# Modulation products of four steps gathered in one row tile before they are turned into columns

## The chip, the cores and the metric

The kernel runs on one core of a Trainium2 chip. The time is the device time of one execution in microseconds (us). The engines are TensorE (PE, with its weight loads shown apart as PEld), VectorE (DVE), ScalarE (ACT), GpSimd (POOL) and SyncE (SP), which issues most DMAs. TensorE writes its results into eight PSUM banks of 128 partitions by 512 fp32 words.

## The reference, cut to what matters

Two blocks are computed one after the other: a first one of two layers (attention with a forget gate, convolutions, feed-forward) over 272 tokens, then a second one whose norms are modulated. The modulation vectors are what this case is about:

```python
N_MOD = 9                       # D_MODEL = 1024
ml = (jax.nn.silu(c) @ ada_w[l] + ada_b[l]).reshape(B, N_MOD, 1, D)
mc = (jax.nn.silu(c_ctx) @ ada_w[l] + ada_b[l]).reshape(N_MOD, 1, 1, D)
x = x + 0.5 * ml[:, 2] * _swiglu(_modulate(_rms(x, ffn1_norm[l]), ml[:, 0], ml[:, 1]), ffn1_w_in[l], ffn1_w_out[l])
h = h + 0.5 * mc[2] * _swiglu(_modulate(_rms(h, ffn1_norm[l]), mc[0], mc[1]), ffn1_w_in[l], ffn1_w_out[l])
...
```

So two vectors of 1024 (silu of c and of c_ctx) are multiplied by a matrix of 1024 x 9216. The rest of the kernel needs the results as columns, 128 features on the partitions: 72 tiles of 128 features, two columns each (tile MOD, seen flat as `modf`).

## The kernel before

Everything is fp32. Each engine has its own hand-written order of instructions; semaphores tie them together (`S.name`), and a small counter class turns them into waits on constants. A matmul of fp32 is two TensorE instructions in the trace.

**Where the modulation is computed.** The matrix of 9216 columns is cut into 18 steps of 512 columns (q = 0 to 17), each fed by two weight strips of 256 columns in the slots W[0] to W[3]. Steps 0 and 1 are in the attention of layer 0, steps 2 and 3 in that of layer 1, steps 4 to 17 in the first feed-forward of the second block (the modulated stage): one after each of its ten product groups and one after each of its four down-projections (`ada(g)`, g = 0 to 13, called as `extra` from `ffn`).

**What a step does.** In `ada_products` (L858) TensorE takes a bank and multiplies, for 8 blocks of 128 features and both strips, the stationary tile CC[:, k, :] of 32 columns by 256 columns of the strip. Only the first two of the 32 columns of CC hold data (written at L1888), the rest are zero. Block k goes to rows 32 * (k % 4) of the bank, so the product lies there in four partial sums of two rows each. `ada_rows` (L1765) on ScalarE copies the bank, 128 x 512, into the row tile AR (two buffers) and gives the bank back. `ada_columns` (L871) on TensorE multiplies each quarter of AR, 128 x 128, as stationary operand by SEL, whose two columns have ones at rows 0, 32, 64, 96 and 1, 33, 65, 97: that adds the partial sums and turns rows into columns, 8 columns in all. `ada_columns` (L1774) on ScalarE copies these into MOD.

**Order around it.** In the feed-forward stage the columns of step 3 + g are turned right after the products of step 4 + g (`ada_turn`, L1204 and L2088), so there the row copy of ScalarE has a whole step of time. In the last, g = 13, the columns of both 16 and 17 are turned. After them TensorE goes on with the sum of squares (`square_sum`, in `stat`, L749), which waits for VectorE's `x2_ready` (set at L2884), and the next norm hangs on it. In the layers both steps' products (L1089, L1090) come before `turn(6)`, and the columns are turned in `turn(6)` and `turn(7)` (L991), ahead of each head's three transposes (L998); ScalarE evicts these in `evict` (L1843, L1844) and then copies the columns (L1776). After `evict(6)` it squares rows (L1858). SyncE loads the output projection (`w_out`) into the same slots as soon as the products have released them. VectorE adds the bias and forms the gains in `modulation(pairs, ...)` (L2413), which first waits for a number of column copies.

Of the kernel before, what the change touches and what calls it, by code (L numbers as in the profile page):

```python
# [28 lines left out]
SW = 256  # L29
# [227 lines left out]
def first_and_second_block(nc, a, out):  # L257
# [4 lines left out]
    with ctx:  # L262
        def sb(name, shape, dt=F32):
            return ctx.enter_context(nc.sbuf_tensor(name, shape, dt))

        S = Semaphores(lambda name: ctx.enter_context(nc.semaphore(name)))
        bank = [ctx.enter_context(nc.psum_tensor(f"bank{b}", [P, 512], F32)) for b in range(8)]


        W = [sb(f"W{r}", [P, SK, SW]) for r in range(SLOTS)]  # L270

        ident = sb("ident", [P, P])
        mean_d = sb("mean_d", [P, P])
        mean_c = sb("mean_c", [P, P])
        mean_g = sb("mean_g", [P, P])
        SEL = sb("SEL", [P, 2])
        eps_rms = sb("eps_rms", [P, 1])
        eps_ln = sb("eps_ln", [P, 1])
        ones_row = sb("ones_row", [P, T1])
# [13 lines left out]
        MOD = sb("MOD", [P, NMOD, KD, 2])  # L293
        GS = sb("GS", [P, 3, KD, 2])
        GATE = sb("GATE", [P, 3, KD, 2])
        CC = sb("CC", [P, KD, 32])
        LBC = sb("LBC", [P, 4, 16])
        NB = sb("NB", [P, 16])
        MQB = sb("MQB", [P, 4])
# [142 lines left out]
        AR = cut(2, 2 * SW)  # L442
# [260 lines left out]
        def _(eng):  # L703
# [9 lines left out]
            def take(b):  # L713
                eng.wait_ge(S.free[b], p.next(S.free[b]))
# [141 lines left out]
                seven_products(n % 2, 4, P, (n % 4,), lambda i: WSM[n % 2][:, i], tokens, lambda i: sums[i],  # L856
                               tokens=each, halves=wait, swap=last)

            def ada_products(b, r):

                take(b)
                for half in range(2):
                    rr = (r + half) % 4
                    eng.wait_ge(S.land[rr], p.next(S.land[rr], 16))
                    for k in range(KD):
                        g = 32 * (k % 4)
                        last = mm(bank[b][g:g + 32, half * SW:(half + 1) * SW], CC[:, k, :], W[rr][:, k, 0:SW],  # L867
                                  start=k < 4, stop=k >= 4, skip_group_check=True)
                    last.then_inc(S.done[rr], p.inc(S.done[rr]))

            def ada_columns(o, q):  # L871

                eng.wait_ge(S.ada_rows, p.next(S.ada_rows))
                for n in range(4):
                    last = mm(o[:, 2 * n:2 * n + 2], AR[:, q % 2, n * P:(n + 1) * P], SEL[:, :], start=True, stop=True,  # L875
                              skip_group_check=True)
                return last

# [65 lines left out]
            for l in range(LAYERS):  # L944
# [46 lines left out]
                def turn(j):  # L991

                    eng.wait_ge(S.p_norm, p.next(S.p_norm))
                    take(6)
                    if j > 5:
                        ada_columns(bank[6][:, 384:392], l * 2 + j - 6)
                    for c in range(3):
                        last = eng.transpose(bank[6][:, c * P:(c + 1) * P], SP[j % 3][:, c * P:(c + 1) * P], ident[:, :])  # L998
                    last.then_inc(S.pt_full, p.inc(S.pt_full))
# [86 lines left out]
                scores(7)  # L1086
                if l == 0:
                    eng.wait_ge(S.cc, p.now(S.cc))
                ada_products(0, 2)  # L1089
                ada_products(1, 0)  # L1090
                turn(6)
                eng.wait_ge(S.vt, p.next(S.vt))
                weigh(2)
# [107 lines left out]
                    if extra:  # L1201
                        extra(10 + u)

            def ada_turn(q):  # L1204

                take(6)
                ada_columns(bank[6][:, 0:8], q).then_inc(S.ada_full, p.inc(S.ada_full))

            def ada(g):

                ada_products(5, 1)
                if g:
                    ada_turn(3 + g)
                if g == 13:
                    ada_turn(17)

            ffn(u2, 2 * SEQ, lambda g: 3 if g else 1, ada)
            square_sum(2 * SEQ)
# [489 lines left out]
        def _(eng):  # L1708
# [53 lines left out]
                    act(sn[:, i, :], bank[b][:, c:c + w], ACT.Copy).then_inc(S.snap, p.inc(S.snap))  # L1762
                p.skip(S.prod, 2)

            def ada_rows(b, r, q):  # L1765

                p.skip(S.done[r % 4])
                r = (r + 1) % 4
                eng.wait_ge(S.done[r], p.next(S.done[r]))
                act(AR[:, q % 2, :], bank[b][:, :], ACT.Copy).then_inc(S.ada_rows, p.inc(S.ada_rows))  # L1770
                eng.wait_ge(S.ada_rows, p.now(S.ada_rows))
                eng.sem_inc(S.free[b], 1)

            def ada_columns(o, q):  # L1774

                act(modf[:, 4 * q:4 * q + 4, :], o.rearrange("p (a b) -> p a b", a=4), ACT.Copy).then_inc(S.mod, p.inc(S.mod))  # L1776
                eng.wait_ge(S.mod, p.now(S.mod))

            for l in range(LAYERS):
# [61 lines left out]
                def evict(j):  # L1841
                    eng.wait_ge(S.pt_full, p.next(S.pt_full))
                    act(PT[:, j, 0:256], bank[6][:, 0:256], ACT.Copy)  # L1843
                    act(PT[:, j, 272:400], bank[6][:, 256:384], ACT.Copy).then_inc(S.pt_ready, p.inc(S.pt_ready))  # L1844
                    eng.wait_ge(S.pt_ready, p.now(S.pt_ready))
                    if j > 5:
                        ada_columns(bank[6][:, 384:392], l * 2 + j - 6)
                    eng.sem_inc(S.free[6], 1)

                def mixed(pair):  # L1850
# [34 lines left out]
                    eng.wait_ge(S.xn, p.next(S.xn))  # L1885
                    act(CS[:, t, :], CV[:, t, :], ACT.Silu, bias=PLs[l][:, C_LNB + t:C_LNB + t + 1]).then_inc(S.cact, p.inc(S.cact))
                if l == 0:
                    act(CC[:, :, 0:2], GS[:, 0, :, :], ACT.Silu).then_inc(S.cc, p.inc(S.cc))  # L1888
                tables(LOG_EXP)
                copies(2, SCX)  # L1890
                evict(2)
# [9 lines left out]
                copies(1, YC[:, 4:6, :])  # L1901
                evict(5)
                exps(7)
                ada_rows(0, 2, l * 2)
                ada_rows(1, 0, l * 2 + 1)
                evict(6)
                eng.wait_ge(S.ysc, p.next(S.ysc, 2))
                head_squares(HK[0:4])
# [176 lines left out]
                if not extra:  # L2085
                    finish(range(6, 8))

            def ada_turn(q):  # L2088

                eng.wait_ge(S.ada_full, p.next(S.ada_full))  # L2090
                ada_columns(bank[6][:, 0:8], q)
                eng.sem_inc(S.free[6], 1)

            def ada(g):

                ada_rows(5, 1, 4 + g)
                if g:
                    ada_turn(3 + g)
                if g == 13:
                    ada_turn(17)  # L2100

            ffn(2 * SEQ, lambda g: 3 if g else 1, 0, 0, ada)
            norm(2 * SEQ, 1, 3)
# [220 lines left out]
        def _(eng):  # L2324
# [22 lines left out]
            def constants():  # L2347

                eng.wait_ge(S.consts, p.next(S.consts))
                eng.memset(maskC[:, 0:SEQ], 0.0)  # L2350
                eng.tensor_reduce(maskC[:, SEQ:T1], H2[:, 0, 0:P].rearrange("p (j c) -> p c j", j=HEADS), AX_X, ALU.add)
                for n, at in enumerate((32, 64, 96)):
                    tt(SEL[:, :], SEL[:, :] if n else ident[:, 0:2], ident[:, at:at + 2], ALU.add).then_inc(S.order_dve, p.inc(S.order_dve))
                    eng.wait_ge(S.order_dve, p.now(S.order_dve))

            def par(c):
# [56 lines left out]
            def modulation(pairs, t0, t1, norm_at=(), gate_at=()):  # L2413

                eng.wait_ge(S.mod, p.next(S.mod, pairs))
                tt(modf[:, t0:t1, :], modf[:, t0:t1, :], P2[:, B_ADA + t0:B_ADA + t1].unsqueeze(2).to_broadcast([P, t1 - t0, 2]), ALU.add).then_inc(S.order_dve, p.inc(S.order_dve))
                eng.wait_ge(S.order_dve, p.now(S.order_dve))
                for n in norm_at:
                    gain, sc = norms_of[n]
                    ts(GS[:, n], MOD[:, sc], 1.0, None, ALU.add).then_inc(S.order_dve, p.inc(S.order_dve))  # L2420
                    eng.wait_ge(S.order_dve, p.now(S.order_dve))
                    tt(GS[:, n], GS[:, n], P2[:, gain:gain + KD].unsqueeze(2).to_broadcast([P, KD, 2]), ALU.mult).then_inc(S.order_dve, p.inc(S.order_dve))
                    eng.wait_ge(S.order_dve, p.now(S.order_dve))
                for n in gate_at:
# [30 lines left out]
            def context():  # L2455

                eng.wait_ge(S.sig, p.next(S.sig))
                tt(LBC[:, 1, :], LBC[:, 2, :], LBC[:, 3, :], ALU.add).then_inc(S.order_dve, p.inc(S.order_dve))
                eng.wait_ge(S.order_dve, p.now(S.order_dve))
                eng.reciprocal(LBC[:, 1, :], LBC[:, 1, :]).then_inc(S.order_dve, p.inc(S.order_dve))  # L2460
                eng.wait_ge(S.order_dve, p.now(S.order_dve))
                tt(LBC[:, 0, :], LBC[:, 2, :], LBC[:, 1, :], ALU.mult).then_inc(S.order_dve, p.inc(S.order_dve))
                eng.wait_ge(S.order_dve, p.now(S.order_dve))
                ts(LBC[:, 1, :], LBC[:, 0, :], -1.0, 1.0, ALU.mult, ALU.add).then_inc(S.order_dve, p.inc(S.order_dve))
                eng.wait_ge(S.order_dve, p.now(S.order_dve))
                modulation(4, 0, 16, norm_at=(0,))

            def context_norm():

# [414 lines left out]
                    eng.memset(tick[:, 0:1], 0.0).then_inc(S.x2_ready, p.inc(S.x2_ready))  # L2884
                    eng.wait_ge(S.x2_ready, p.now(S.x2_ready))

            ffn(2 * SEQ, lambda g: 3 if g else 1, 0, lambda: modulation(8, 16, 48, norm_at=(1,), gate_at=(0, 1)))
            norm(2 * SEQ, 1)
            modulation(6, 48, 72, norm_at=(2,), gate_at=(2,))

            for k in range(KD):
                eng.wait_ge(S.u, p.next(S.u))
# [369 lines left out]
```

## Time and profile before

| | |
|---|---|
| Median of 3 runs | 2059.34 us (2059.31 to 2059.37) |
| The profiled execution | 2057.46 us |
| its span, first to last instruction | 2055.7 us |
| mean granted clock | 0.998 of full speed |

TensorE is busy for 98% of the span by the page. The page gives each engine's busy time, the chain of work that ended last, and the costliest groups of instructions. A chain is followed back from the last instruction: at each step to whatever released it, or to the instruction before it on its engine. The waits list who waited for whom. The timeline merges instructions of one line that follow each other: start, duration, engine, line, operation, output tile and inputs, count, and in brackets the idle time of the engine before it and what ended it. Two timeline rows of TensorE can overlap slightly, since a matmul's end is pipelined under the next one; starts are the better measure.

### The profile page before, as it was taken

The page shows a single profiled execution, that of the slowest core. Times are in us where ns is not written, and L with a number is a line of the kernel's source. Part 1 is how long each engine was busy: PE and PEld are TensorE (multiplying, and loading weights), DVE is VectorE, ACT ScalarE, POOL GpSimd, SP SyncE. Part 2 cuts the span into 40 slices and gives each one's busy share as a digit, 9 for nine tenths or more (in the row PEclk, how much of TensorE's full clock was granted, in tenths as well). Part 3 has the DMA queues.
Part 4 walks back from the last instruction along what each step waited for, and adds up shares of the span by engine and source line. Part 5 has one row for each costly group of instructions (what it writes and reads, how often), then busy time and mean ns, then how long its engine had stood idle before and what let it go on. Part 6 is the DMA issues. An engine that isn't in the chain of part 4 may idle for free.

```text
span 2055.7 us, 31756 instructions
## 1 busy us (share of the span) xinstructions
PE 2023.5 (98%) x12969; PEld 1806.3 (88%) x12969; DVE 1079.0 (52%) x2170; ACT 569.3 (28%) x1366; POOL 175.9 (9%) x232
## 2 busy tenths in 40 slices
PE   9999999999999999999999999999999999999998
PEld 7868999977789998888888888888889889999998
DVE  5424987571278865333336235333245545776664
ACT  3344332223433313111111004322332323232212
POOL 5110340312013300000000001000000000000000
PEclk9999999999999999999999999999999999999999
DMA  6244454342444543444455336422212214444552
GB/s 191 95 156 146 165 171 155 107 145 97 159 162 146 194 134 101 151 145 152 149 172 167 98 100 193 128 85 83 82 62 82 62 54 131 165 144 165 172 182 77
DMA packets 274874, 273.63 MB, mean 133 GB/s; under 512 B 11023, under 2 KB 272379, under 8 KB 274731
## 3 DMA queue, kind: packets, MB, share of 16 engines
q1 hardware_dynamic: 272920, 267.65, 40.2%
q0 software_dynamic: 1216, 3.32, 0.5%
q8 instruction: 103, 1.69, 0.3%
q10 hardware_dynamic: 594, 0.65, 0.1%
q14 instruction: 41, 0.33, 0.0%
HBM read 270.38 MB, written 1.08 MB: 132 GB/s over the span
## 4 chain that ended last, share of the span: by engine, by line
PE 94%; DVE 3%; ACT 1%; DMA 1%; issue 1%; SPq 0%; DVEq 0%; ACTq 0%
PE bank L782 50%; PE bank L1224 11%; PE bank L769 8%; PE bank L1403 5%; PE bank L910 3%; PE bank L1417 2%; PE bank L969 2%; PE bank L1021 1%; PE bank L867 1%; PE bank L1468 1%; PE bank L1389 1%; PE bank L1430 1%; DMA W<-in_ada_w_dram 1%; PE bank L875 1%; PE bank L980 1%; PE bank L1156 1%
## 5 line engine op out<-in xcount | busy, mean ns | idle before, releaser
L782 PE MATMUL bank<-arena,SQ 128*128 128x136 f32 (+2 forms) x2176 | 341.5, 308 | 2.6 <-ACT arena L1762 2.6
L782 PEld LDWEIGHTS bank<-arena,SQ 128*128 128x128 f32 x2176 | 307.0, 191 | 19.8 <-ACT arena L1762 2.8
L782 PE MATMUL bank<-arena,W 128*128 128x136 f32 (+2 forms) x1824 | 272.6, 301 | 2.3 <-issue 2.1
L782 PEld LDWEIGHTS bank<-arena,W 128*128 128x128 f32 x1824 | 247.7, 191 | 13.6 <-issue 2.4
L1762 ACT ACTIVATE H<-bank 128x128 f32<-128x128 f32 (+1 forms) x260 | 82.4, 317 | 508.9 <-PE bank L782 508.8
L782 PE MATMUL bank<-U,W 128*128 128x136 f32 (+2 forms) x1296 | 194.4, 303 | 0.0
L782 PEld LDWEIGHTS bank<-U,W 128*128 128x128 f32 x1296 | 176.5, 191 | 8.5 <-issue 0.4
L769 PE MATMUL bank<-U,W 128*128 128x272 f32 (+2 forms) x608 | 140.6, 392 | 2.4 <-DVEq L2409 1.2
L769 PEld LDWEIGHTS bank<-U,W 128*128 128x128 f32 (+1 forms) x608 | 111.7, 185 | 30.0 <-issue 3.9
L782 PE MATMUL bank<-arena 128*128 128x136 f32 (+1 forms) x1024 | 124.1, 278 | 0.0
L782 PEld LDWEIGHTS bank<-arena 128*128 128x128 f32 x1024 | 120.6, 191 | 0.0
L2552 DVE TENSOR_TENSOR arena<-H,bank 128x128 f32<-128x128 f32 (+1 forms) x57 | 19.1, 334 | 160.1 <-ACT H L1762 160.1
L1224 PE MATMUL bank<-W,U 128*128 128x256 f32 (+1 forms) x512 | 100.5, 355 | 0.0
L782 PE MATMUL bank<-U,SQ 128*128 128x136 f32 (+2 forms) x608 | 98.2, 304 | 0.0
L1224 PEld LDWEIGHTS bank<-W,U 128*128 128x128 f32 x512 | 86.8, 190 | 11.5 <-issue 2.0
L1762 ACT ACTIVATE arena<-bank 128x136 f32<-128x136 f32 x176 | 49.2, 280 | 169.5 <-PE bank L782 169.5
L782 PEld LDWEIGHTS bank<-U,SQ 128*128 128x128 f32 x608 | 85.9, 191 | 4.1
L1224 PE MATMUL bank<-arena 128*128 128x256 f32 (+3 forms) x352 | 66.2, 332 | 0.0
L1674 POOL TENSOR_TENSOR SQ<-W 128x512 f32<-128x512 f32 x32 | 40.8, 1276 | 279.4 <-PE bank L782 279.4
L1224 PEld LDWEIGHTS bank<-arena 128*128 128x128 f32 (+2 forms) x352 | 52.2, 179 | 14.1 <-issue 4.0
L2703 DVE SCALAR_TENSOR_TENSOR arena<-arena,PL 128x270 f32<-128x270 f32 x72 | 61.8, 858 | 2.6
L910 PE MATMUL bank<-arena,W 128*128 128x272 f32 x256 | 60.3, 394 | 1.7 <-ACT arena L1752 1.7
(418 smaller groups left out, 3052.4 us busy)
## 6 DMA issues: line engine op xcount, KB each, us to landing
W<-in_ffn_w_up_dram SPq DMA_DIRECT2D x44, 1024.0 KB, 5.0
W<-in_ffn_w_in_dram SPq DMA_DIRECT2D x44, 1024.0 KB, 5.0
W<-in_ada_w_dram SPq DMA_DIRECT2D x36, 1024.0 KB, 6.5
W<-in_mix_w_in_dram SPq DMA_DIRECT2D x36, 1024.0 KB, 5.3
W<-in_w_in_dram SPq DMA_DIRECT2D x22, 1024.0 KB, 5.1
W<-in_ffn_w_down_dram SPq DMA_DIRECT2D x16, 1408.0 KB, 6.4
W<-in_ffn_w_out_dram SPq DMA_DIRECT2D x16, 1408.0 KB, 6.0
W<-in_w_out_dram SPq DMA_DIRECT2D x8, 1024.0 KB, 8.1
```

The costliest lines, as they stand in the source:

```text
L769: last = mm(bank[b][0:m, 0:n], W[r][:, kk, t * P:t * P + m], rhs(kk), start=kk == 0, stop=kk == k - 1)
L782: last = mm(o, a(k), b[:, k], start=not adds and k == 0, stop=k == kt - 1, skip_group_check=True)
L867: last = mm(bank[b][g:g + 32, half * SW:(half + 1) * SW], CC[:, k, :], W[rr][:, k, 0:SW], start=k < 4, stop=k >= 4, skip_group_check=True)
L875: last = mm(o[:, 2 * n:2 * n + 2], AR[:, q % 2, n * P:(n + 1) * P], SEL[:, :], start=True, stop=True, skip_group_check=True)
L910: return mm(bank[2 * (r % 2) + t][:, c0:c0 + n], W[r][:, k, t * P:(t + 1) * P], rhs(k), start=k == 0, stop=k == KD - 1, skip_group_check=True)
L969: last = mm(o, U[:, kk, t0:t0 + w], W[r][:, kk, 0:SW], start=kk == 0, stop=kk == KD - 1)
L1224: last = mm(o, x, y, start=i == 0, stop=i == n - 1 and bias is None, skip_group_check=True)
L1403: last = mm(bank[b][:, c:c + SEQ], W[r][:, k, t * P:(t + 1) * P], src[:, k, c:c + SEQ], start=k == 0, stop=k == KD - 1, skip_group_check=True)
L1417: last = mm(bank[b][:, c:c + SW], tok(k), W[r][:, k, :], start=k == 0, stop=k == KD - 1, skip_group_check=True)
L1674: eng.tensor_tensor(WS[n % 2][:, 0], part(1, 0), part(1, 1), ALU.add).then_inc(S.order_pool, p.inc(S.order_pool))
L1762: act(sn[:, i, :], bank[b][:, c:c + w], ACT.Copy).then_inc(S.snap, p.inc(S.snap))
L2703: stt(CZ[:, i, 2:], Z[:, g % 2, i, 0:T1 - 2], w(0), CZ[:, i, 2:], ALU.mult, ALU.add).then_inc(sem, p.inc(sem))
```

## The change

Up to four steps now add into one bank. Step i of a group of n uses CC shifted by two columns, so that its data fall on rows 2 i and 2 i + 1 of every group of 32; only the very first products carry the start flag. CC grows to 38 columns with the data in columns 6 and 7, SEL to 8 columns. One copy of the bank into AR then carries n steps, and one turning gives 8 n columns in four matmuls of 2 n. In the layers the two steps form one group, turned with head 7. In the feed-forward stage the groups are steps 0 to 3, 4 to 7, 8 to 11 and 12, 13 (g), turned in steps 4, 8, 12 and 13. The last is turned right after its own products.

```diff
-        SEL = sb("SEL", [P, 2])
+        SEL = sb("SEL", [P, 8])
-        CC = sb("CC", [P, KD, 32])
+        CC = sb("CC", [P, KD, 38])
...
-            def ada_products(b, r):
-
-                take(b)
+            def ada_products(b, r, i, n):
+
+                if i == 0:
+                    take(b)
                 for half in range(2):
                     rr = (r + half) % 4
                     eng.wait_ge(S.land[rr], p.next(S.land[rr], 16))
                     for k in range(KD):
                         g = 32 * (k % 4)
-                        last = mm(bank[b][g:g + 32, half * SW:(half + 1) * SW], CC[:, k, :], W[rr][:, k, 0:SW],
-                                  start=k < 4, stop=k >= 4, skip_group_check=True)
+                        last = mm(bank[b][g:g + 32, half * SW:(half + 1) * SW], CC[:, k, 6 - 2 * i:38 - 2 * i], W[rr][:, k, 0:SW],
+                                  start=i == half == 0 and k < 4, stop=i == n - 1 and k >= 4, skip_group_check=True)
                     last.then_inc(S.done[rr], p.inc(S.done[rr]))
-            def ada_columns(o, q):
+            def ada_columns(o, a, n):
                 eng.wait_ge(S.ada_rows, p.next(S.ada_rows))
-                for n in range(4):
-                    last = mm(o[:, 2 * n:2 * n + 2], AR[:, q % 2, n * P:(n + 1) * P], SEL[:, :], start=True, stop=True,
+                for j in range(4):
+                    last = mm(o[:, 2 * n * j:2 * n * (j + 1)], AR[:, a, j * P:(j + 1) * P], SEL[:, 0:2 * n], start=True, stop=True,
                               skip_group_check=True)
...
-                    if j > 5:
-                        ada_columns(bank[6][:, 384:392], l * 2 + j - 6)
+                    if j == 7:
+                        ada_columns(bank[6][:, 384:400], 0, 2)
...
-                ada_products(0, 2)
-                ada_products(1, 0)
+                ada_products(0, 2, 0, 2)
+                ada_products(0, 0, 1, 2)
...
             def ada(g):
-                ada_products(5, 1)
-                if g:
-                    ada_turn(3 + g)
+                ada_products(5, 1, g % 4, 2 if g > 11 else 4)
+                if g in (4, 8, 12):
+                    ada_turn(g // 4 - 1, 4)
                 if g == 13:
-                    ada_turn(17)
+                    ada_turn(3, 2)
...
-            def ada_rows(b, r, q):
-
-                p.skip(S.done[r % 4])
-                r = (r + 1) % 4
-                eng.wait_ge(S.done[r], p.next(S.done[r]))
-                act(AR[:, q % 2, :], bank[b][:, :], ACT.Copy).then_inc(S.ada_rows, p.inc(S.ada_rows))
+            def ada_rows(b, slots, a):
+
+                for r in slots:
+                    eng.wait_ge(S.done[r], p.next(S.done[r]))
+                act(AR[:, a, :], bank[b][:, :], ACT.Copy).then_inc(S.ada_rows, p.inc(S.ada_rows))
...
-                    if j > 5:
-                        ada_columns(bank[6][:, 384:392], l * 2 + j - 6)
+                    if j == 7:
+                        ada_columns(bank[6][:, 384:400], l * 2, 2)
...
-                ada_rows(0, 2, l * 2)
-                ada_rows(1, 0, l * 2 + 1)
+                ada_rows(0, (2, 3, 0, 1), 0)
...
             def ada(g):
-                ada_rows(5, 1, 4 + g)
-                if g:
-                    ada_turn(3 + g)
+                if g in (3, 7, 11):
+                    p.skip(S.done[1], 3)
+                    p.skip(S.done[2], 3)
+                    ada_rows(5, (1, 2), g // 4 % 2)
+                elif g == 13:
+                    p.skip(S.done[1])
+                    p.skip(S.done[2])
+                    ada_rows(5, (1, 2), 1)
+                if g in (4, 8, 12):
+                    ada_turn(g // 4 - 1, 4)
                 if g == 13:
-                    ada_turn(17)
+                    ada_turn(3, 2)
...
-                modulation(4, 0, 16, norm_at=(0,))
+                modulation(2, 0, 16, norm_at=(0,))
...
-            ffn(2 * SEQ, lambda g: 3 if g else 1, 0, lambda: modulation(8, 16, 48, norm_at=(1,), gate_at=(0, 1)))
+            ffn(2 * SEQ, lambda g: 3 if g else 1, 0, lambda: modulation(2, 16, 48, norm_at=(1,), gate_at=(0, 1)))
             norm(2 * SEQ, 1)
-            modulation(6, 48, 72, norm_at=(2,), gate_at=(2,))
+            modulation(2, 48, 72, norm_at=(2,), gate_at=(2,))
```

## Rows read from the trace of the kernel before

**Rows 1.** The page: the chain that ended last, by engine.

```profile
PE 94%; DVE 3%; ACT 1%; DMA 1%; issue 1%; SPq 0%; DVEq 0%; ACTq 0%
```

**Rows 2.** Groups by line and shape: count, busy us, mean ns, idle before.

```profile
L875 PE MATMUL bank<-SEL,arena 128*128 128x2 f32 x144 | 18.8, 252 | 0.3 <-ACTq L2092 0.3
...
L867 PEld LDWEIGHTS bank<-W,CC 128*32 128x32 f32 x576 | 16.9, 109 | 17.0 <-issue 5.3 <-DMA W<-in_ada_w_dram 2.4
```

**Rows 3.** All waits of TensorE from 840 to 1235 us.

```profile
PE bank L875 <- ACTq L2092: 0.3, 1, 0.3
```

**Rows 4.** Timeline of TensorE, the first three steps of the modulated stage.

```profile
841.17 1.93 PE L867 MATMUL bank<-W,CC 128*32 128x256 f32 x32
843.03 3.72 PE L782 MATMUL bank<-U,W 128*128 128x256 f32 x16
...
867.40 1.93 PE L867 MATMUL bank<-W,CC 128*32 128x256 f32 x32
869.27 1.05 PE L875 MATMUL bank<-SEL,arena 128*128 128x2 f32 x8
870.18 3.70 PE L782 MATMUL bank<-U,W 128*128 128x256 f32 x16
...
894.53 1.93 PE L867 MATMUL bank<-W,CC 128*32 128x256 f32 x32
```

**Rows 5.** The chain in order of time, a down-projection step (start us, us, what).

```profile
1122.56 0.98 PE bank L875 x8
```

**Rows 6.** Timeline of all engines, end of the modulated stage.

```profile
1229.20 1.93 PE L867 MATMUL bank<-W,CC 128*32 128x256 f32 x32
1231.07 1.05 PE L875 MATMUL bank<-SEL,arena 128*128 128x2 f32 x8
1231.20 0.60 ACT L1770 ACTIVATE arena<-bank 128x512 f32<-128x512 f32 x1 [11.01 <-PE bank L867]
...
1232.43 1.06 PE L875 MATMUL bank<-SEL,arena 128*128 128x2 f32 x8 [0.31 <-ACTq L2092]
1232.62 0.06 DVE L2884 MEMSET tick<- 128x1 f32 x1
...
1233.35 2.06 PE L749 MATMUL bank<-SQ,mean_d 128*128 128x512 f32 x2
```

**Rows 7.** The chain in order of time, layer 0 (start us, us, what).

```profile
130.34 1.07 PE bank L867 x16
131.41 0.98 PE bank L875 x8
132.39 0.40 PE bank L998 x3
...
132.81 0.38 ACT arena L1843
...
133.40 0.19 ACT MOD L1776
...
133.69 1.39 ACT SQ L1858 x4
```

**Rows 8.** Timeline, layer 0: ScalarE's copy of the rows.

```profile
131.47 0.60 ACT L1770 ACTIVATE arena<-bank 128x512 f32<-128x512 f32 x1 [2.43 <-PE bank L867]
```

**Rows 9.** The chain in order of time, layer 1.

```profile
517.59 0.98 PE bank L875 x8
```

**Rows 10.** Groups by line and shape: unaligned moving columns, and aligned ones.

```profile
L1224 PE MATMUL bank<-arena 128*128 128x129 f32 x96 | 19.2, 309 | 0.0
...
L1446 PE MATMUL bank<-arena 128*128 128x128 f32 x32 | 4.2, 275 | 0.0
```

**Rows 11.** Output projection in layer 0: second load, first use; all eight loads' landing.

```profile
128.44 0.37 SPq L567 DMA_DIRECT2D W<-in_w_out_dram  x1
...
139.12 1.08 PE L1021 MATMUL bank<-arena,W 128*128 128x272 f32 x4
...
DMA to landing us min/median/max: 5.5/8.1/11.7
```

More of the change, by code:

```diff
@@ L1202, in ffn, with ada_turn @@
                         extra(10 + u)
-            def ada_turn(q):
+            def ada_turn(g, n):
                 take(6)
-                ada_columns(bank[6][:, 0:8], q).then_inc(S.ada_full, p.inc(S.ada_full))
+                ada_columns(bank[6][:, 0:8 * n], g % 2, n).then_inc(S.ada_full, p.inc(S.ada_full))
             def ada(g):
-                ada_products(5, 1)
-                if g:
-                    ada_turn(3 + g)
+                ada_products(5, 1, g % 4, 2 if g > 11 else 4)
+                if g in (4, 8, 12):
+                    ada_turn(g // 4 - 1, 4)
                 if g == 13:
-                    ada_turn(17)
+                    ada_turn(3, 2)
             ffn(u2, 2 * SEQ, lambda g: 3 if g else 1, ada)
@@ L1763, in snapshots, with ada_columns @@
                 p.skip(S.prod, 2)
-            def ada_rows(b, r, q):
-                p.skip(S.done[r % 4])
-                r = (r + 1) % 4
-                eng.wait_ge(S.done[r], p.next(S.done[r]))
-                act(AR[:, q % 2, :], bank[b][:, :], ACT.Copy).then_inc(S.ada_rows, p.inc(S.ada_rows))
+            def ada_rows(b, slots, a):
+                for r in slots:
+                    eng.wait_ge(S.done[r], p.next(S.done[r]))
+                act(AR[:, a, :], bank[b][:, :], ACT.Copy).then_inc(S.ada_rows, p.inc(S.ada_rows))
                 eng.wait_ge(S.ada_rows, p.now(S.ada_rows))
                 eng.sem_inc(S.free[b], 1)
-            def ada_columns(o, q):
-                act(modf[:, 4 * q:4 * q + 4, :], o.rearrange("p (a b) -> p a b", a=4), ACT.Copy).then_inc(S.mod, p.inc(S.mod))
+            def ada_columns(o, q, n):
+                act(modf[:, 4 * q:4 * (q + n), :].rearrange("p (i j) c -> p j i c", j=4),
+                    o.rearrange("p (j i c) -> p j i c", j=4, i=n), ACT.Copy).then_inc(S.mod, p.inc(S.mod))
                 eng.wait_ge(S.mod, p.now(S.mod))
@@ L1887, in _ @@
                 if l == 0:
-                    act(CC[:, :, 0:2], GS[:, 0, :, :], ACT.Silu).then_inc(S.cc, p.inc(S.cc))
+                    act(CC[:, :, 6:8], GS[:, 0, :, :], ACT.Silu).then_inc(S.cc, p.inc(S.cc))
                 tables(LOG_EXP)
@@ L2086, in ffn, with ada_turn @@
                     finish(range(6, 8))
-            def ada_turn(q):
+            def ada_turn(g, n):
                 eng.wait_ge(S.ada_full, p.next(S.ada_full))
-                ada_columns(bank[6][:, 0:8], q)
+                ada_columns(bank[6][:, 0:8 * n], 4 + 4 * g, n)
                 eng.sem_inc(S.free[6], 1)
             def ada(g):
-                ada_rows(5, 1, 4 + g)
-                if g:
-                    ada_turn(3 + g)
+                if g in (3, 7, 11):
[8 more added lines that the diff above has]
+                    ada_turn(g // 4 - 1, 4)
                 if g == 13:
-                    ada_turn(17)
+                    ada_turn(3, 2)
             ffn(2 * SEQ, lambda g: 3 if g else 1, 0, 0, ada)
@@ L2352, in constants @@
                 for n, at in enumerate((32, 64, 96)):
-                    tt(SEL[:, :], SEL[:, :] if n else ident[:, 0:2], ident[:, at:at + 2], ALU.add).then_inc(S.order_dve, p.inc(S.order_dve))
+                    tt(SEL[:, :], SEL[:, :] if n else ident[:, 0:8], ident[:, at:at + 8], ALU.add).then_inc(S.order_dve, p.inc(S.order_dve))
                     eng.wait_ge(S.order_dve, p.now(S.order_dve))
```

## The prediction

> **What bounds the kernel now.** I read the page first: TensorE carries 94% of the chain that ended last [rows 1]. So time goes away only where TensorE does less, or where a chain that TensorE waits for gets shorter. Next I looked for the two kinds of instruction that the change touches. The products of the modulation (L867) are 576 TensorE instructions, the turning into columns (L875) is 144 [rows 2]: 18 groups of 8, since each of the 4 matmuls of a group is two instructions. Are those groups on the path? The waits of TensorE inside the modulated feed-forward stage hold one entry, 0.3 us [rows 3]. Everything else there runs back to back, so whatever is taken out of TensorE's order should come out of the time. The timeline gives the price: in the first step, which has no turning, the products start at 841.17 and the next matmul at 843.03, 1.86 us. In the next step they start at 867.40, the turning at 869.27 (1.87 later) and the next matmul at 870.18: 0.91 us for the turning [rows 4]. The start-up gap of 0.4 us after the products is paid with or without it. In a down-projection step, which is longer, the chain passes through a turning of the same size, 0.98 us with its handover [rows 5]. Two such groups lie in each of the two layers' attention, where the chain runs partly through ScalarE [rows 7 to 9].
>
> **Part 1, the feed-forward stage: turnings taken out.** Before, a turning follows in steps 1 to 13, and a second one in step 13: 14 groups. After, there are groups in steps 4, 8, 12 and 13 only. Steps 1, 2, 3, 5, 6, 7, 9, 10 and 11 lose theirs: 9 x 0.91 = 8.2 us. In the period of a step (867.40 to 894.53, less 841.17 to 867.40) the difference is 0.90, so I take 8.1 [rows 4]. The remaining groups move 4 or 8 columns for 2. A matmul of 129 columns takes 309 ns and one of 2 takes 252 [rows 2, 10], so six more columns are worth about 3 ns if they are seen at all: nothing. That the products now add onto what is there (no start flag) changes nothing in their number or size.
>
> Is there a cover that goes away with the turning? Weights are loaded and summed beside TensorE. The first step is the test: it already runs without a turning and the next matmul starts at once [rows 3, 4]. A DMA or a VectorE sum that was only just in time would show there. ScalarE is spared 10 evictions of rows there and waits less in its order; it was not on the path.
>
> **Part 2, the end of that stage.** Here a group is removed, but it was cover. Before: products start at 1229.20, ScalarE's copy of the rows starts at 1231.20 and takes 0.60, and meanwhile TensorE turns the group of the step before (1231.07), then waits 0.31 for the bank and turns the last one (1232.43). The squares' sum (L749) starts at 1233.35 [rows 6]. After: TensorE has nothing to do while ScalarE copies. The copy ends at 1231.80, the turning can start at 1231.9 with a handover of under 0.1, and L749 at 1231.9 + 0.91 = 1232.8. Queued behind this new wait on TensorE is L749 alone, and it also waits for VectorE's flag, set at 1232.62 + 0.06 [rows 6]: the two come together, at 1232.8. Gain 0.5 us instead of the 1.3 that one group and its wait would suggest. Past L749 the norm and all that follows hang on it and move with it.
>
> **Part 3, the layers.** In each layer the chain runs: fourth weight strip lands, 16 products (1.07), turning (0.98), three transposes (0.40), then ScalarE's evictions from 132.81, the copy of the columns (0.19) at 133.40, the squares from 133.69 [rows 7]. After, turning and column copy are gone from head 6, and head 7 has one of each, as before. But ScalarE now comes to its eviction through the one copy of the rows, which needs all four strips: it starts at 131.47, takes 0.60 and ends at 132.07 [rows 8]; the transposes, moved up by 0.98, end before that, at 131.8. So the eviction starts at about 132.15 instead of 132.81 (0.66), and without the column copy (0.19 and 0.03 of issue) the squares start 0.88 us earlier. Layer 1 repeats the pattern, turning 0.98 in the chain [rows 9]: 2 x 0.88 = 1.8 us. Behind the merged wait ScalarE has only head 6's eviction, which comes after the same products anyway. The next thing that could be late is the output projection: its weights are asked for at 128.44 (second strip), and such strips land in 8.1 us at the median [rows 11], about 136.5, against a first use at 139.1 that would become 138.2. The slowest of the eight takes 11.7 us, but that can't be the second strip, which would have come a full microsecond too late before. I cost it at nothing; without this cover up to the whole 0.88 of a layer is lost.
>
> **Part 4, the shifted tile.** The left operand of all 576 product instructions now starts 0 to 24 bytes further on, with rows of 38 words instead of 32. Whether such a weight load is slower, no row shows. The nearest rows are moving operands that start at odd multiples of 129 words: 309 ns against 275 for an aligned 128 columns [rows 10], so at most 34 ns, and that mean also holds other causes. The lower bound is zero: nothing in the change makes an aligned load slower than it can be, and nothing gains. I take zero, because at 1.86 us for 32 instructions (58 ns each) [rows 4] four column groups of the array work side by side and the matmul's 256 columns, not the 32 of the load, set the pace.
>
> The Trainium skill speaks against the shift: "SBUF — State Buffer", section "Door 1: The DMA port swizzle", says that accesses which cross into a new 16-byte line pay. 32 words that start 8 bytes into a line touch nine lines instead of eight; estimated from that page, an eighth more of a load. By it a 110 ns load would cost 14 ns more, 8 us in all if nothing hid it, and nearly all of the gain would go. No row of before shows it; it belongs to the second rival below.
>
> **Sum.** 8.1 + 0.5 + 1.8 = 10.4 us; constants and the wider selector on VectorE add some hundredths, 10.3 remain. The profiled execution took 2057.46 us (span 2055.7 and 1.8 around it) and would come to 2047.2. The runs' median of before is 2059.34, 1.9 above the profiled one; I predict against the median: 2049.0 us, 0.5% faster.
>
> **Rivals.**
> - Only the plain removals pay (chance 0.12). The layers' gain is eaten by a wait that takes its place (output weights, ScalarE), and the end gains nothing: 8.1 us, 2051.2. For it: 1.8 us hang on a chain over three engines. Against: each link of that chain was released by the one before, not by a DMA [rows 7].
> - The shifted loads cost something (0.07). At a tenth of the 34 ns it is 576 x 3.4 ns = 2.0 us, 2051.0; at half 9.8 us, 2058.8, which counts as no change. Against: the load lies under the matmul.
> - The shifted loads cost the full 34 ns of the nearest row (0.03): 576 x 0.034 = 19.6 us, less 10.3: 9.3 slower, 2068.6. The balance turns at 10.3 / 576 = 18 ns per instruction. 34 is more than half of the 58 ns pace, so it could not hide.
> - That the change doesn't do what it says is excluded by the text: the groups are counted in the order of instructions, 18 become 6.
> - Everything as summed: 0.78.
>
> **How the numbers follow.** Likeliest 2049.0. Its own range is 2047.2 (the runs of after lie like the profiled one) to 2050.3. The range of 8 in 10 takes in the first rival and the cheap end of the second, with 0.7 more for how far runs of two occasions lie apart: 2046.8 to 2052.0. A measurement of this kernel can tell about 0.2% (4 us) from no change. Faster by more than that: 0.78 + 0.12 + 0.03 of the second rival = 0.93. Within: 0.04. Slower: 0.03.
>
> **What the profile of after would show.** L875 x48 in place of x144. In the feed-forward stage the period of steps without turning is 26.2 us and with it 27.1, with the pace of L867 still 1.86 us for 32. Near the end one wait of TensorE at L875 for ScalarE's L1770 (0.8 us or so). In the layers L1858's first square 2.5 us after the start of the last 16 products, instead of 3.35. The prediction is wrong if L867's spacing grows, if TensorE waits for a weight DMA where it had none, or if a step without turning is longer than the first step of before.

## The result, and the profile after

| | before | after |
|---|---|---|
| Median of 5 runs | 2059.34 us (2058.65 to 2060.75) | 2049.24 us (2048.69 to 2049.87) |
| The profiled execution | 2057.46 us | 2048.82 us |
| its span | 2055.7 us | 2047.1 us |

The ratio of after to before is 0.9949, with a 95% interval of 0.9937 to 0.9961: 10.1 us faster by the medians, 8.6 us by the two traces. The chain of the page, by engine, is nearly what it was [rows 1]:

```profile
PE 95%; DVE 2%; ACT 1%; DMA 1%; issue 1%; POOL 0%; DVEq 0%; SPq 0%; ACTq 0%; POOLq 0%
```

The turnings are 48 instructions in place of 144 and the products are as many and as long as before [rows 2]. By tile, with minimum, median and maximum in ns (the line numbers of TensorE's instructions are one higher after):

```profile
L876 PEld LDWEIGHTS bank<-SEL,arena x48: 186/192/192, 135.6 to 1224.9; 128*128 128x128 f32 x48
L876 PE MATMUL bank<-SEL,arena x48: 169/254/277, 135.9 to 1224.9; 128*128 128x4 f32 x24, 128*128 128x8 f32 x24
...
L868 PEld LDWEIGHTS bank<-W,CC x576: 105/110/110, 126.5 to 1222.7; 128*32 128x32 f32 x192
L868 PE MATMUL bank<-W,CC x576: 379/379/404, 126.5 to 1222.9; 128*32 128x256 f32 x192
```

The timeline of TensorE in the modulated stage, to be held against [rows 4]:

```profile
841.37 1.93 PE L868 MATMUL bank<-W,CC 128*32 128x256 f32 x32
843.23 3.72 PE L782 MATMUL bank<-U,W 128*128 128x256 f32 x16
...
867.60 1.94 PE L868 MATMUL bank<-W,CC 128*32 128x256 f32 x32
869.47 3.72 PE L782 MATMUL bank<-U,W 128*128 128x256 f32 x16
...
893.84 1.93 PE L868 MATMUL bank<-W,CC 128*32 128x256 f32 x32
```

From one start of the products to the next there are 26.23 and 26.24 us (867.60 less 841.37, then 893.84 less 867.60), where before there were 27.13 from the second step on. The next matmul comes 1.86 to 1.87 us after the products start. From the first products of the stage to the last it is 379.99 us (841.37 to 1221.36) instead of 388.03 (841.17 to 1229.20): 8.04 us less, 0.89 for each of nine turnings.

The end of the stage, all engines, against [rows 6]:

```profile
1221.36 1.93 PE L868 MATMUL bank<-W,CC 128*32 128x256 f32 x32
...
1223.43 0.60 ACT L1770 ACTIVATE arena<-bank 128x512 f32<-128x512 f32 x1 [11.07 <-PE bank L868]
...
1224.17 1.03 PE L876 MATMUL bank<-SEL,arena 128*128 128x4 f32 x8 [0.87 <-ACT arena L1770]
1224.78 0.06 DVE L2891 MEMSET tick<- 128x1 f32 x1
...
1225.06 1.10 PE L749 MATMUL bank<-SQ,mean_d 128*128 128x512 f32 x2
1225.23 0.18 ACT L1776 ACTIVATE MOD<-bank 128x16 f32<-128x16 f32 x1 [1.21 <-PE bank L876]
1225.52 1.28 ACT L1719 ACT_TABLE_LOAD   x1
...
1226.82 0.47 ACT L2027 ACTIVATE LNT<-bank,eps_rms 128x256 f32<-128x256 f32 x1
```

TensorE now waits 0.87 us for ScalarE's copy of the rows, as foreseen; the squares' sum starts 3.70 us after the last products instead of 4.15. VectorE's flag was set 0.2 us before. ScalarE loads its table only after it has copied the columns, and the norm's first operation (L2027, 1226.82) starts right behind that load (1225.52 + 1.28), not when the squares' sum is done, which is 0.66 us earlier (1225.06 + 1.10).

In layer 1 the chain in order of time is, against [rows 7, 9]:

```profile
515.86 1.11 PE bank L868 x16
...
517.08 0.61 ACT arena L1770
...
518.46 1.39 ACT SQ L1859 x4
...
524.04 1.38 PE bank L1022 x6
```

The turning is gone from it and the copy of the rows stands there: 2.60 us from the last 16 products to the first square instead of 3.35 [rows 7]. Layer 0 repeats it to 0.01 us, with the products 0.45 us later in this execution (130.79), since the strip landed later.

These pieces are worth 8.04 + 0.45 + 2 x 0.75 = 10.0 us, but the two traces differ by 8.6. Most of the rest is TensorE's clock. Stretches of time, with each engine's busy time in them, the granted clock, DMA share and GB/s, first of before and then of after:

```profile
1233.30:1234.30 1.00, 1.00 (x3) 0.53 (x3) 0.00 (x0) 0.67 (x2) 0.00 (x0) 0.53 0.32 106
1234.30:1235.20 0.90, 0.90 (x3) 0.34 (x2) 0.00 (x0) 0.79 (x1) 0.00 (x0) 0.50 0.73 182
```

```profile
644.00:645.00 1.00, 1.00 (x7) 1.00 (x6) 0.93 (x3) 0.00 (x0) 0.00 (x0) 0.50 0.00 0
645.00:646.00 1.00, 1.00 (x6) 1.00 (x6) 0.97 (x2) 0.28 (x1) 0.00 (x0) 0.50 0.00 0
...
1225.00:1226.00 1.00, 1.00 (x5) 0.52 (x5) 0.00 (x0) 0.67 (x2) 0.00 (x0) 1.00 0.08 27
```

Before has a stretch at the lower level (0.50 of 2.4 GHz, so 1.2 GHz) at the end of the stage and none around 645; after has it the other way round. VectorE's instructions come 1.4 us earlier than before at 523 us, in layer 1's attention, and 0.2 us later at 649, in its feed-forward: 1.6 us went there, in work that the change doesn't touch. The stretch of before lies in the piece from the last products to the next projection (L1224, after L1225), which is 16.60 us before and 15.77 after: 0.83 less, where the squares' start gained 0.45. Whether these stretches belong to the change is a question for the experiments.

One more difference lies near 400 us, between the layers, where the change edits nothing: ScalarE's L1724 (before L1723), the first operation of a norm, starts 0.72 us after the start of TensorE's second sum of squares, in place of 1.00. It does so in all eight traces of kernels built from after, the one that groups the stage only among them, and in none of the four built from before. Its cause is open. With it the account of the two traces closes: 8.04 + 0.83 + 2 x 0.75 + 0.3, less 1.6 at 645 us and 0.45 for the late strip, is 8.6.

### The profile page after: what moved, and what is told of

Read it like the earlier page. It is cut to its first block, busy times and chain, and to the rows that moved or that the text cites. A ratio compares the mean times of both kernels' runs of the same rounds, so it can differ in the third digit from the quotient of the medians.

```text
span 2047.1 us, 31504 instructions
## 1 busy us (share of the span) xinstructions
PE 2013.2 (98%) x12873; PEld 1796.3 (88%) x12873; DVE 1078.6 (53%) x2170; ACT 560.0 (27%) x1342; POOL 175.8 (9%) x232
## 4 chain that ended last, share of the span: by engine, by line
PE 95%; DVE 2%; ACT 1%; DMA 1%; issue 1%; POOL 0%; DVEq 0%; SPq 0%; ACTq 0%; POOLq 0%
PE bank L782 51%; PE bank L1225 11%; PE bank L769 8%; PE bank L1404 5%; PE bank L911 3%; PE bank L1418 3%; PE bank L970 2%; PE bank L1469 2%; PE bank L1022 1%; PE bank L868 1%; PE bank L1390 1%; PE bank L1431 1%; DMA W<-in_ada_w_dram 1%; PE bank L981 1%; PE bank L1157 1%; PE bank L1163 1%
## 5 line engine op out<-in xcount | busy, mean ns | idle before, releaser
L1225 PE MATMUL bank<-W,U 128*128 128x256 f32 (+1 forms) x512 | 100.5, 355 | 0.0
L1225 PEld LDWEIGHTS bank<-W,U 128*128 128x128 f32 x512 | 86.8, 190 | 11.5 <-issue 2.0
L1225 PE MATMUL bank<-arena 128*128 128x256 f32 (+3 forms) x352 | 66.2, 332 | 0.0
L1225 PEld LDWEIGHTS bank<-arena 128*128 128x128 f32 (+2 forms) x352 | 52.2, 179 | 14.1 <-issue 4.0
```

The lines of the kernel that those rows point to most:

```text
L1225: last = mm(o, x, y, start=i == 0, stop=i == n - 1 and bias is None, skip_group_check=True)
```

## The experiments

**Which part gives what.** The first kernel groups the modulated stage only, the second the layers only. From the kernel after, the first puts back:

```diff
-                    if j == 7:
-                        ada_columns(bank[6][:, 384:400], 0, 2)
+                    if j > 5:
+                        ada_columns(bank[6][:, 384:392], j - 6, 1)
...
-                ada_products(0, 2, 0, 2)
-                ada_products(0, 0, 1, 2)
+                ada_products(0, 2, 0, 1)
+                ada_products(1, 0, 0, 1)
...
-                ada_rows(0, (2, 3, 0, 1), 0)
+                ada_rows(0, (2, 3), 0)
+                ada_rows(1, (0, 1), 1)
```

and the second, in the stage on TensorE and likewise on ScalarE:

```diff
-                ada_products(5, 1, g % 4, 2 if g > 11 else 4)
-                if g in (4, 8, 12):
-                    ada_turn(g // 4 - 1, 4)
-                if g == 13:
-                    ada_turn(3, 2)
+                ada_products(5, 1, 0, 1)
+                if g:
+                    ada_turn(g - 1, 1)
+                if g == 13:
+                    ada_turn(13, 1)
```

> Only the modulated stage is grouped (steps of 4, 4, 4 and 2); the layers turn their steps one by one, as before. Theory (removed work): the stage gives 9 turnings of 0.90 us and 0.45 us at its end, about 8.5 us against before. Rival A (the gain is spread evenly over the 12 removed groups, the layers' two among them): 10 of 12, 8.4 us; the split can't tell A apart here, the layers' run does. Rival B (the stage's gain is given back later, because VectorE or a DMA is late next): under 5 us. The profile should show the starts of the products 26.23 us apart in steps without a turning and 27.13 with one.

> Only the layers are grouped; the modulated stage turns every step, as before. Theory (the trace of after: from the last 16 products to the first square 2.60 us instead of 3.35): 0.75 us in each layer, 1.5 us in all. Rival A (a removed turning is worth 0.9 us wherever it lies): 1.8 us. Rival B (the merged copy of the rows or the output weights take the gain back): 0. By the times alone 1.5 and 0 are hard to tell apart; the distance from the last 16 products to the first use of the output weights in each layer decides.

The stage alone: 2050.99 us against 2059.21, ratio 0.9963 (0.9950 to 0.9975), 8.2 us by the medians and 5.1 to 10.3 by the interval; the theory's 8.5 holds and rival B (under 5) falls, though not by much. The layers alone: 2059.15, ratio 1.0000 (0.9992 to 1.0009), so the time shows nothing, and its interval excludes neither 1.5 us nor nothing. The chain of its layer 1 does show it:

```profile
517.11 1.11 PE bank L868 x16
...
519.71 1.39 ACT SQ L1859 x4
...
525.29 1.38 PE bank L1022 x6
```

2.60 us to the first square and 8.18 us to the output projection's products, as in after (518.46 and 524.04 less 515.86), where before has 3.36 and 8.94:

```profile
516.51 1.07 PE bank L867 x16
...
519.87 1.39 ACT SQ L1858 x4
...
525.45 1.38 PE bank L1021 x6
```

So 0.76 us a layer is shown in the traces; that it arrives in the time rests on the sum only. Neither the output weights nor the merged copy took it back.

**Does the shifted tile cost anything?** This was the unknown with the widest bounds.

```diff
-        CC = sb("CC", [P, KD, 32])
+        CC = sb("CC", [P, KD, 39])
-                        last = mm(bank[b][g:g + 32, half * SW:(half + 1) * SW], CC[:, k, :], W[rr][:, k, 0:SW],
+                        last = mm(bank[b][g:g + 32, half * SW:(half + 1) * SW], CC[:, k, 7:39], W[rr][:, k, 0:SW],
-                    act(CC[:, :, 0:2], GS[:, 0, :, :], ACT.Silu).then_inc(S.cc, p.inc(S.cc))
+                    act(CC[:, :, 7:9], GS[:, 0, :, :], ACT.Silu).then_inc(S.cc, p.inc(S.cc))
```

> The kernel before, but the left operand of the 576 product instructions lies in rows of 39 words and starts at word 7, so no load starts on a 16-byte boundary except by chance of the row. Nothing else changes. Theory (the load hides under the matmul): no change in time, 32 products still start 1.86 us before the next matmul. Rival (a load that straddles one more line is slower): up to 14 ns each, 8 us slower, and the 32 products take up to 2.3 us.

2059.42 us, ratio 1.0003 (0.9994 to 1.0012), and the timeline of TensorE:

```profile
844.47 1.93 PE L867 MATMUL bank<-W,CC 128*32 128x256 f32 x32
846.33 3.72 PE L782 MATMUL bank<-U,W 128*128 128x256 f32 x16
```

Still 1.86 us for 32, and the profile's own time of such a load is 109 ns at the mean in this trace, as in before [rows 2] and in after. So the load isn't slower here, and it isn't only hidden. The rival's 8 us are outside the interval; a loss of 2 us would not be, but the spacing excludes that too. The Trainium skill's sentence on 16-byte lines ("SBUF — State Buffer", section "Door 1: The DMA port swizzle") doesn't show in this form of load, in this kernel or in after.

**The price of a turning by itself.**

```diff
-            def ada_columns(o, q):
+            def ada_columns(o, q, times=1):
                 eng.wait_ge(S.ada_rows, p.next(S.ada_rows))
-                for n in range(4):
+                for n in times * tuple(range(4)):
...
-                ada_columns(bank[6][:, 0:8], q).then_inc(S.ada_full, p.inc(S.ada_full))
+                ada_columns(bank[6][:, 0:8], q, 2).then_inc(S.ada_full, p.inc(S.ada_full))
```

> The kernel before, but each turning in the modulated stage is done twice in a row (8 matmuls, 16 instructions in place of 8, with one wait). It measures the price of a turning by itself. Theory: TensorE bound, 14 x 0.8 to 0.9 us more, 11 to 13 us slower; the step from one turning's start to the next matmul 1.7 to 1.8 us instead of 0.91. Rival (what a turning costs is the change of the kind of work around it, not its eight instructions): a second one behind the first costs much less, under 7 us in all.

2073.37 us, ratio 1.0072 (1.0059 to 1.0086): 14.2 us more by the medians, and 12.1 to 17.7 by the interval. The timeline of TensorE:

```profile
870.48 1.95 PE L875 MATMUL bank<-SEL,arena 128*128 128x2 f32 x16
872.29 3.70 PE L782 MATMUL bank<-U,W 128*128 128x256 f32 x16
```

1.81 us for two, so the second costs 0.90 like the first, and 14 of them 12.6. The price is that of the eight instructions, and not of the change of the kind of work. Each has a load of 128 x 128 weights and, as the wider turnings below show, the number of columns behind it (2 to 16) doesn't matter. That the load sets the price is inferred: no run changes it alone. The Trainium skill gives a load as its columns divided by 1.2, in ns ("TensorE: Matmul & The Clock Gate", section "LDWEIGHTS (loading the stationary operand)"), an estimate of 107 ns or 0.85 us for eight. The trace's spacing of 0.90 us for eight is near it; the records of the single loads, which overlap the matmuls, last 192 ns.

**Removed or moved?** In the layers, is the gain that of a turning less, or of one that no longer stands ahead of head 6?

```diff
-                    if j > 5:
-                        ada_columns(bank[6][:, 384:392], l * 2 + j - 6)
+                    if j == 7:
+                        ada_columns(bank[6][:, 384:392], l * 2)
+                        ada_columns(bank[6][:, 392:400], l * 2 + 1)
```

(on TensorE in `turn`, and the same on ScalarE in `evict`, from the kernel before).

> The kernel before, but in each layer both single turnings come with head 7 (two copies of the rows and two turnings remain). It tells a removed turning from a moved one. Theory (at head 6 a turning lies on the chain, at head 7 it lies beside ScalarE's chain with 0.21 us to spare): from the last 16 products to the first square 2.6 us instead of 3.35, but then 0.91 - 0.21 = 0.7 us more before the first use of the output weights, so that the distance from the last 16 products to that use (8.9 us in the trace of before) stays within 0.1. Rival (head 7 has room): that distance falls to 8.2 us, as in the trace of after, and the change's gain in the layers would be had by moving alone.

My theory fell. Layer 1's chain:

```profile
517.69 1.11 PE bank L867 x16
...
520.23 0.44 ACT SQ L1860
...
522.87 1.68 PE bank L875 x16
...
525.86 1.38 PE bank L1022 x6
```

8.17 us to the output projection, against 8.94 before and 8.18 after; in layer 0 it is 8.16. Two turnings stand in this chain (1.68 us): TensorE's own order now sets the time, and it reaches the projection no later than ScalarE's chain does in after. I had counted 0.21 us of slack behind head 7. But the way from the first turning of head 7 to the projection is, by the timeline, 3.15 us with two turnings (522.71 to 525.86) and 3.10 before with one (522.35 to 525.45), so nearly the whole second turning fits into TensorE's waits there; one of them, 0.34 us at a later square, I had left out. Moving alone gives what merging gives in the layers. The time, 2057.84 us in one execution, can't tell 1.5 us.

**Further in the same direction.** Two more turnings less: groups of 8 and 6 in the stage.

```diff
-                ada_products(5, 1, g % 4, 2 if g > 11 else 4)
-                if g in (4, 8, 12):
-                    ada_turn(g // 4 - 1, 4)
+                ada_products(5, 1, g % 8, 6 if g > 7 else 8)
+                if g == 8:
+                    ada_turn(0, 8)
                 if g == 13:
-                    ada_turn(3, 2)
+                    ada_turn(1, 6)
```

(CC with 46 columns, SEL with 16, ScalarE and VectorE to match.)

> The kernel after, but the modulated stage's 14 steps form groups of 8 and 6 (rows 0 to 15 of each 32). Two more turnings fall away, those in steps 4 and 12. Theory (price 0.90 each): 1.8 us below the kernel after, 11.5 to 12 below the one before. Rival (wider turnings, 16 columns for 8, or a copy that now carries 8 steps, cost what is saved): no change against after.

2048.96 us where before ran at 2060.85 beside it, ratio 0.9938 (0.9925 to 0.9951). After's interval overlaps, so the time alone doesn't separate them. The turning of eight steps:

```profile
1054.40 1.06 PE L876 MATMUL bank<-SEL,arena 128*128 128x16 f32 x8
1055.32 0.89 PE L782 MATMUL bank<-U,W 128*128 128x256 f32 x3
```

0.92 us with 16 columns a matmul, for 0.91 with 2. Held against after's trace, the same instructions come 0.9 us earlier from each of the two removed places on.

**The end of the stage.** ScalarE's table load was behind the last turning, so that turning was put behind the squares' sum:

```diff
             def ada(g):
...
-                if g == 13:
-                    ada_turn(3, 2)
...
             square_sum(2 * SEQ)
+            ada_turn(3, 2)
```

(and on ScalarE after the norm's exponentials).

> The kernel after, but the last turning follows the sum of squares on TensorE, and ScalarE copies its columns after the norm's two exponentials. Theory (at the end of the stage the table load of ScalarE stands behind the turning and its copy; free of them it starts 1.4 us earlier and the norm starts when the squares' sum is done): 0.5 to 0.7 us faster than after. Rival (TensorE then idles 1.6 us in one piece for VectorE's flag and its granted clock falls to half behind it): the squares' sum takes 2.1 us instead of 1.1, and the gain turns into a loss of about 0.5 us.

2050.15 us, ratio 0.9946 (0.9935 to 0.9958): again not separable from after by time. From the last products (1222.77) to the projection it is 15.26 us instead of 15.77 (1221.36 to 1237.13 in after):

```profile
1226.39 1.10 PE L749 MATMUL bank<-SQ,mean_d 128*128 128x512 f32 x2 [1.69 <-DVE tick L2890]
...
1238.03 3.62 PE L1224 MATMUL bank<-U,W 128*128 128x256 f32 x16
```

0.5 us as expected, and no stretch at half clock after 1.69 us of idle time. ScalarE's first operation of the norm (L2026) now waits 0.71 us for the squares' sum: the path has changed over to that sum. In before's code it was the table load. The same place in the odd tile's kernel, whose clock is full there:

```profile
1236.65 1.10 PE L749 MATMUL bank<-SQ,mean_d 128*128 128x512 f32 x2
...
1237.10 1.28 ACT L1718 ACT_TABLE_LOAD   x1
...
1238.40 0.47 ACT L2027 ACTIVATE LNT<-bank,eps_rms 128x256 f32<-128x256 f32 x1
```

In this one trace the gain doesn't last: at 1279.42 TensorE waits 0.84 us at L1224 for something that the profile doesn't show, and the traces of after and of the last kernel below, which has the same late turning, have no such wait.

**The idle time that the slow stretch of after follows.** In layer 1's feed-forward TensorE waits 2.6 us for ScalarE, which waits for VectorE, which does 3.4 us of work on parameters. Part of that work was moved three groups on:

```diff
+            def lower_bounds():
+
...
                         p.count.update(counted)
+                    if l and g == 7:
+                        lower_bounds()
```

> The kernel after, but in layer 1's feed-forward VectorE does the arithmetic on the second block's parameters (lower bounds, about 2.2 us of its 3.4 us there) three groups later than the copy of the parameters. It touches the place where the trace of after lost 1.6 us against before. Theory (TensorE idles 2.6 us there for ScalarE, which waits for VectorE, and in some executions its granted clock is at half for the next microseconds): the idle time falls to about 0.4 us, no stretch at half clock follows it, 2.2 us faster plus what the clock costs on average, 2.2 to 3.8 in all. Rival (the two things have nothing to do with each other): the idle time falls, the half-clock stretch stays at the same place. Rival B (the parameters' work just stalls TensorE three groups later): no gain.

2049.96 us, ratio 0.9948 (0.9933 to 0.9963): no gain. The wait of 2.6 us became 0.41 there and one three groups later, which is rival B:

```profile
641.32 1.19 PE L782 MATMUL bank<-arena,SQ 128*128 128x136 f32 x8 [0.41 <-ACT arena L1763]
...
682.56 1.19 PE L782 MATMUL bank<-arena,SQ 128*128 128x136 f32 x8 [2.06 <-ACT arena L1763]
```

The moved work holds up VectorE, and TensorE behind it, in its new place too. No stretch at half clock followed here; one execution doesn't say why (below).

**After again, and both improvements together.**

> The kernel after, unchanged, beside the next kernel on the same chip. Theory (its 10 us are 9 removed turnings, 1.5 us in the layers and 0.4 at the end of the stage; the stretches at half clock differ from execution to execution and lie on top): within 1 us of 10.1 below before; in its trace the last products start 15.8 us before the projection's first matmul, whatever the clock does elsewhere. Rival (part of the 10 us was luck of the executions timed first): 8 us or less.

> Groups of 8 and 6 in the modulated stage, and the last turning after the sum of squares with its columns copied after the norm's exponentials. Theory (both traces add up: 1.8 us for two more turnings, 0.5 us at the end of the stage, 15.3 us instead of 15.8 from the last products to the projection): 2.3 us below after, near 2047. Rival (the longer idle time of TensorE before the squares brings a stretch at half clock, and the wider turnings are no cheaper): no difference from after.

After again: 2048.76 us, ratio 0.9941 (0.9929 to 0.9953), 11.3 us by the medians. That is 0.2 more than the theory's 1 us around 10.1 allows, on the far side from the rival, and the interval begins at 9.7: the rival falls. From the last products to the projection it is 15.76 us, as foreseen. The trace has no stretch at half clock until the last 5 us, and a span of 2045.2 us: 10.5 below the span of before, whose own stretch at 1234 us accounts for 0.4 of that (below). That leaves 10.1 for the change: 10.0 in the pieces and 0.3 near 400 us, less 0.2 since the strips of the two layers landed later.

Both together: 2047.93 us, ratio 0.9942 (0.9930 to 0.9954), span 2044.3. By the medians 0.8 us below after, within the noise of both. The traces show the 2.3 to 2.4 us: against the trace of after again the same instructions come 0.9 and 0.9 earlier at the two removed turnings and 0.6 at the end of the stage, but 1.3 us of it went to a stretch at half clock around 643 us. I call it a version that its trace shows as better and the time doesn't contradict, no more.

## Why the prediction was right

The median of after, 2049.24 us, is 0.2 us from the forecast. Step by step:

- **Part 1** (nine turnings, 8.1): 8.04 in the trace, and the price of 0.90 was confirmed by doubling it. That the first step, without a turning, could stand for all others was the reading that carried the most, and it held in every step. Wider turnings cost 0.01 us at most (0.92 for 0.91, with 16 columns).
- **Part 2** (the end, 0.5): the start of the squares gained 0.45. From the last products to the projection, in traces without a slow stretch, it is 16.20 us with before's code (the odd tile's kernel, 1232.50 to 1248.70) and 15.77 after: 0.43. The copy started 2.07 us after the products and not 2.00, which is the difference. The path was not the forecast's, though: it let the norm hang on the squares' sum, while in the traces at full clock it hangs on ScalarE's table load, 0.66 us later (odd tile's kernel 0.65). The load follows the last copy of columns, which follows the last turning, as the squares' sum does too. Both came 0.45 us earlier for that reason, and so the number held by luck.
- **Part 3** (the layers, 2 x 0.88): mis-sized, 0.76. The term that was off is the start of the copy of the rows: 1.22 us after the last 16 products start, not the 1.13 of [rows 7, 8], and its end hands over to the eviction in 0.11 us, where I had put 0.08. What pays there is that head 6 is free of its turning; that one turning is also gone altogether adds nothing, as the moved turnings showed. The output weights were no hindrance.
- **Part 4** (the shifted tile, nothing within 0 to 34 ns): nothing, and the rivals that rested on it, at 0.07 and 0.03, are gone. The reason given, that the load lies under the matmul, wasn't needed: the load itself took no longer (109 ns). The bound of 34 ns came from moving operands and was no bound for this kind of load; it only widened the range.
- **Against its own time**: the forecast for the profiled execution was 2047.2, and it came out at 2048.82, 1.6 too high. The forecast took the clock for the same in both. The stretch at 645 us is worth those 1.6 us; the smaller differences nearly cancel.

The forecast on the median was closer than its parts deserve. The sum of the measured pieces is 10.0, 0.3 less than I had, the 0.3 near 400 us were in no part of it, and the medians gave 10.1 and later 11.3.

## What to carry to other kernels

On an engine that runs back to back, look for a repeat of the loop that lacks the piece to be removed: its period is the forecast, and it shows whether anything was hiding behind the piece. A matmul with few moving columns has a price that doesn't depend on their number, here up to 16, so gather work for it in rows until the tile is full. Before giving a removal its full price on a chain over several engines, ask whether moving it to a place with slack would do as well, and add up all waits behind that place, not the first. A fitting number doesn't prove the path: look which of two waits ends last.

## What the runs showed of the hardware

TensorE's granted clock falls to half (1.2 GHz) for about 3.4 us at a few places of this kernel, not in every execution. Twelve traces (two of them of the kernel after) show it at three places before the last 15 us:

- near 14 us, in 7 of 12, in work that all of them share;
- near 645 us, behind a 2.6 us idle time of TensorE: in 7 of the 11 that have that idle time in one piece, about 1.4 to 1.7 us lost each time;
- at the end of the modulated stage: in 4 of the 5 kernels that end it with two or more turnings in a row, and in none of the 7 that have one there. It is worth less than it looks: 16.60 us from the last products to the projection with the stretch (before), 16.20 without (the odd tile's kernel), 0.4 us, because ScalarE's chain covers the rest.

What TensorE did before the clock fell at the last place were, in before, 16 instructions of two columns each over 2.3 us, with 0.3 us of waiting; 1.7 us of pure idle time there (the two kernels with the late turning) brought no fall, nor did 2.06 us at 682 us (the moved parameters). That the turnings caused it is suggested by 4 of 5 against 0 of 7, and not shown by an experiment of its own. For reading: two traces of this kernel can differ by 3 us for this reason alone, so distances between two events of one stage, with the clock's row beside them, are the measure, and not the spans.
